# Up-to-down seams, opening orders and first combinations of a seven-product feed-forward kernel in exact-split fp32 on one core

## The reference

```
x = x + 1/2 * swiglu_ffn(rms(x)); x = x + mixer(rms(x)); x = x + 1/2 * swiglu_ffn(rms(x))   # per layer
swiglu_ffn(x) = (silu(gate) * up) @ w_out      with gate, up = split(x @ w_in), hidden width 2816
mixer of layer 0: pointwise projection + GLU, causal depthwise conv (31 taps), layer norm, swish, projection
mixer of layer 1: differential attention with rotary, over K and V computed from x after layer 0
y = rms(x)
```

## Time and profile before

| what | value |
|---|---|
| runs | 2136.56, 2140.81, 2141.0 us |
| profiled execution | 2139.42 us, its span 2137.6 us |
| PE busy | 1957.2 us (92%), 15236 matmuls |
| DVE, ACT, POOL busy | 1439.6 (67%), 868.9 (41%), 342.1 us (16%) |
| DMA | 340.70 MB, mean 159 GB/s |
| chain that ended last | PE 54%, DVE 24%, ACT 9%, issue 6%, DMA 5% |

### The profile page before, as it was taken

One profiled execution on the slowest core, in us unless ns is written; L12 is line 12 of the kernel. 1 busy time (PEld: TensorE's weight loads), 2 busy tenths in 40 slices (PEclk: granted clock), 3 DMA queues, 4 the chain that ended last, 5 costly groups with the idle time before them and its releaser, 6 DMA issues.

```text
span 2137.6 us, 36366 instructions
## 1 busy us (share of the span) xinstructions
PE 1957.2 (92%) x15236; PEld 1871.0 (88%) x15236; DVE 1439.6 (67%) x1739; ACT 868.9 (41%) x1235; POOL 342.1 (16%) x343
## 2 busy tenths in 40 slices
PE   4999899899789899899997999999988989998996
PEld 4989899888588899899997999899965779898996
DVE  6766757699867648566655747557678567567475
ACT  5423424455554324233344424333356445234242
POOL 1101000133121001011421001010421221010001
PEclk9999999999899999999999999999999999999998
DMA  9758566278457477573559568573676266584651
GB/s 265 165 148 216 139 171 157 78 158 168 92 143 192 115 191 169 151 196 81 155 147 244 134 171 194 158 177 90 190 227 227 79 159 147 165 219 119 176 146 55
DMA packets 318783, 340.70 MB, mean 159 GB/s; under 512 B 12163, under 2 KB 279812, under 8 KB 318476
## 3 DMA queue, kind: packets, MB, share of 16 engines
q1 hardware_dynamic: 275460, 216.97, 32.2%
q0 software_dynamic: 33840, 111.21, 27.7%
q10 hardware_dynamic: 9320, 10.20, 1.6%
HBM read 221.58 MB, written 7.53 MB: 107 GB/s over the span
## 4 chain that ended last, share of the span: by engine, by line
PE 54%; DVE 24%; ACT 9%; issue 6%; DMA 5%; ACTq 1%; POOL 0%; POOLq 0%; DVEq 0%; SPq 0%
PE ps_all L670 27%; PE ps_all L642 24%; DVE w_lo L1379 6%; ACT w_hi L999 4%; DVE conv_b L1655 2%; DVE t_gate L1502 2%; DVE conv L1655 2%; DMA raw<-w_out 1%; DMA raw_more_low<-raw_more_low 1%; DMA raw<-raw 1%; DVE xs_lo_low L1408 1%; DVE t_out L1533 1%; DVE t_gate L1446 1%; DVE hs_lo_low L1538 1%; DVE x L1611 1%
## 5 line engine op out<-in xcount | busy, mean ns | idle before, releaser
L670 PE MATMUL ps_all<-xs_hi_low,w_hi 128*128 128x260 f32 x1848 | 531.6, 288 | 60.1 <-DVE w_lo L1379 34.0
L670 PE MATMUL ps_all<-xs_hi_low,w_lo 128*128 128x260 f32 x1848 | 527.1, 285 | 0.0
L670 PE MATMUL ps_all<-xs_lo_low,w_hi 128*128 128x260 f32 x1848 | 524.7, 284 | 0.0
L999 ACT ACTIVATE w_hi<-raw 128x1024 fp32r<-128x1024 f32 (+1 forms) x252 | 259.0, 1028 | 463.8 <-PE ps_all L642 189.0
L670 PEld LDWEIGHTS ps_all<-xs_hi_low,w_hi 128*128 128x128 f32 x1848 | 352.2, 191 | 68.4 <-DVE w_lo L1379 41.2
L1379 DVE TENSOR_TENSOR w_lo<-raw,w_hi 128x1024 fp32r<-128x1024 f32 (+1 forms) x252 | 315.7, 1253 | 125.2 <-ACT w_hi L999 124.6
L670 PEld LDWEIGHTS ps_all<-xs_lo_low,w_hi 128*128 128x128 f32 x1848 | 352.3, 191 | 0.1
L670 PEld LDWEIGHTS ps_all<-xs_hi_low,w_lo 128*128 128x128 f32 x1848 | 352.0, 190 | 0.0
L999 ACT ACTIVATE w_hi<-raw_more_low 128x1024 fp32r<-128x1024 f32 x156 | 164.6, 1058 | 298.7 <-PE ps_all L670 194.6
L1379 DVE TENSOR_TENSOR w_lo<-raw_more_low,w_hi 128x1024 fp32r<-128x1024 f32 x156 | 192.3, 1238 | 104.1 <-ACT w_hi L999 103.8
L642 PE MATMUL ps_all<-hs_hi_low,w_hi 128*128 128x260 f32 x1056 | 222.2, 292 | 43.3 <-DVE hs_lo_low L1538 43.3
(11 more groups left out here) (251 smaller groups left out, 3624.7 us busy)
## 6 DMA issues: line engine op xcount, KB each, us to landing
raw_more_low<-w_in SPq DMA_DIRECT2D x105, 512.0 KB, 7.1
raw<-w_in SPq DMA_DIRECT2D x80, 512.0 KB, 6.1
raw_more_low<-raw_more_low POOLq DMA_DIRECT2D x72, 512.0 KB, 6.6
raw<-w_out SPq DMA_DIRECT2D x64, 512.0 KB, 4.8
raw<-raw POOLq DMA_DIRECT2D x60, 512.0 KB, 7.8
raw_more_high<-w_in SPq DMA_DIRECT2D x35, 512.0 KB, 7.0
raw<-w_out SPq DMA_DIRECT2D x32, 384.0 KB, 3.4
raw_more_high<-raw_more_high POOLq DMA_DIRECT2D x24, 512.0 KB, 6.4
```

The source lines that it names most:

```text
L670: mm = nc.tensor.matmul(ps_all[:, bank, 0:HALF], w[:, ring, j * GW + q * P:j * GW + (q + 1) * P], m, start=j == 0 and k == 0, stop=j == PA ...
L999: nc.scalar.activation(w_hi[:, n % RING, 0:width], src, ACT.Copy).then_inc(hi_made, 1)
```

## The change

1. **Down phases open with two tiles held back**: chunks 0 and 1 without their last two hidden tiles, then those two of each (`down_ramp`).
2. **The last group by token halves**: gate, Silu, product, high and low part run for the first 260 tokens between items 3 and 6, for the second behind item 6. `gate_first` moves ahead of `hidden_lo` and of `step(n + 3)` in all groups.
3. **First combinations in two places**: for FFN 0 pairs 1 and 3 use a second stage; squares, their sums and lambda move between the items of the first group.
4. **Orders**: `root` and `rms` of a fresh up phase move to items 3 and 4, the variance's PSUM to banks 0 and 1, so that item 5 waits for `rstd`; EARLY is 7; the last `step` of a down phase comes ahead of its drain; in `conv_out`, `o` and `v` the low part of a pair comes one step later; W12 of f=2's first group gets a buffer of its own and is loaded second.

```diff
-        ps_stat_up = ps_all[:, 6:8, 0:HALF]
+        ps_stat_up = ps_all[:, 0:2, 0:HALF]
...
+        stage_2, = over(XG + 108160, KD * T * 4, [("stage_2", [P, 8, HALF])])
+        w12_first, = over(XG + 62464, KD * P * 4, [("w12_first", [P, KD * P])])
+        def stage_of(s, j):
+            return stage_2 if s == 0 and j % 2 else stage
...
-                for blk in (W11, S3, S1, W22, W12) if first_in else (S3, S1, W22, W11, W12):
+                for blk in (W11, W12, S3, S1, W22) if first_in else (S3, S1, W22, W11, W12):
...
-        EARLY = 5
+        EARLY = 7
...
-                        if ph.kind == "up" and ph.part == 0 and ph.f == 2 and c == 4:
+                        if ph.kind == "up" and ph.part == 0 and ph.f == 2 and c == 5:
                             sp.wait_ge(chunk_used, ph.chunk0)
...
-                        hi, lo, ready = room.h_hi[:, k], room.h_lo[:, k], (h_ready, ph.h0 - ph.tiles + k + 1)
+                        hi, lo, ready = room.h_hi[:, k], room.h_lo[:, k], (h_ready, ph.h0 - ph.tiles + k // 2 * 2 + 2)
...
                     elif i == 5:
                         pe.wait_ge(p1_copied, ph.group0 + g + 1)
+                        if g == 0 and fresh(ph):
+                            pe.wait_ge(rstd_made, made + 1)
...
-                            if fresh(ph):
-                                variance(sums, (rstd_made, made) if made else None, ps_stat_up)
...
-                            if i == 3 and g == 0 and ph.part == 0:
-                                pe.wait_ge(rstd_made, made + fresh(ph))
-                                if ph.f == 2:
-                                    pe.wait_ge(v_copied, KD)
+                            if i == 3 and g == 0 and fresh(ph):
+                                variance(sums, (p1_copied, ph.group0 + 1), ps_stat_up)
+                            elif i == 3 and g == 0 and ph.part == 0:
+                                pe.wait_ge(v_copied, KD)
...
+                def down_ramp():
+                    early, late = range(ph.tiles - 2), range(ph.tiles - 2, ph.tiles)
+                    for tiles in (early, late):
+                        for c in range(2):
+                            chunk(ph, c, tiles=tiles)
...
+                first, second, last = slice(0, HALF), slice(HALF, T), ph.groups - 1
                 for g in range(ph.groups):
                     for i in range(ITEMS):
                         step(ph.chunk0 + ITEMS * g + i)
+                        if ph is phases[0] and g == 0:
+                            first_work(i)
                         if g and i == 1:
                             silu(g - 1)
                         elif g and i == 2:
                             hidden_hi(g - 1)
-                        elif not g and i == 1 and fresh(ph):
+                        elif not g and i == 3 and fresh(ph):
                             root(ps_stat_up)
+                        elif g == last and i == 4:
+                            silu(g, first, 1)
+                        elif g == last and i == 6:
+                            hidden_hi(g, first, 1)
                         if i == 1:
                             copy_p1(g)
-                silu(ph.groups - 1)
-                hidden_hi(ph.groups - 1)
+                silu(last, second, 1)
+                hidden_hi(last, second, 1)
...
+            def pair_before_lo(s, m):
+                if m and m % 2 == 0:
+                    combos_lo(s, m // 2 - 1, 0, 7, m // 2)
...
                     step(n + 1)
+                    if opening:
+                        first_work(1)
                     if g:
                         hidden(g - 1)
-                    elif fresh(ph):
-                        rms(ps_stat_up)
                     step(n + 2)
-                    if g:
-                        hidden_lo(g - 1)
-                    step(n + 3)
...
                     gate_first(g)
+                    if g:
+                        hidden_lo(g - 1)
+                    step(n + 3)
...
+                    if g == last:
+                        gate(g, first, 1)
                     step(n + 4)
+                    if g == 0 and fresh(ph):
+                        rms(ps_stat_up)
                     thirds(g)
                     step(n + 5)
                     up_second(g)
+                    if g == last:
+                        up_first(g)
+                        hidden(g, first, 1)
                     step(n + 6)
-                    up_first(g)
-                g = ph.groups - 1
-                gate_second(g)
-                gate(g)
-                hidden(g)
-                hidden_lo(g)
+                    if g == last:
+                        hidden_lo(g, first, 1)
+                    else:
+                        up_first(g)
+                gate_second(last)
+                gate(last, second, 1)
+                hidden(last, second, 1)
+                hidden_lo(last, second, 1)
...
-                    if m < KD - 1:
-                        step(n)
+                    step(n)
+                    if s in (2, 6):
+                        pair_before_lo(s, m)
                     dve.wait_ge(chunk_used, n + 1)
```

More of the change, by code:

```diff
@@ L434, in block_of @@
         def block_of(ph, g, block):
+            if ph.f == 2 and ph.part == 0 and g == 0 and block == W12:
+                return w12_first[:, :]
             return raw_of(ph, block + 5 * in_second(ph, g))
@@ L1063, in _, with first_work @@
             act.wait_ge(vec_in, 16)
[L1064 to L1069, removed]
-            round_hi(1)
[L1071 to L1078, removed]
+            act.wait_ge(x_in[0], 16)
+            copy_x(0, 0)
+            copy_x(0, 1)
+            act.wait_ge(x_in[1], 16)
+            copy_x(0, 2)
+            copy_x(0, 3)
+            combos_hi(0, 0, 0, 7, 4, 2)
+            round_hi(0)
+            combos_hi(0, 1, 0, 7, 4, 2)
+            act.wait_ge(x_in[2], 16)
+            pair_hi(0, 4)
+            pair_hi(0, 5)
+            round_hi(1)
+            act.wait_ge(x_in[3], 16)
+            pair_hi(0, 6)
+            pair_hi(0, 7)
+            def first_work(i):
+                if i < 2:
+                    for m in range(4 * i, 4 * i + 4):
+                        first_square(m)
+                elif i == 2:
+                    act.wait_ge(inputs, N_IN)
+                    nc.scalar.activation(ident_b[:, :], cst[:, C_ID:C_ID + P], ACT.Copy).then_inc(mask_made, 1)
+                    nc.scalar.activation(mask_b[:, :], cst[:, C_MASK:C_MASK + P], ACT.Copy).then_inc(mask_made, 1)
+                    act.wait_ge(lam_step, 2)
+                    nc.scalar.activation(lam_s[0:1, 2:4], lam_s[0:1, 0:2], ACT.Exp).then_inc(lam_step, 1)
+                    act.dma_start(new_state_d, state[:, 1:CW - 1, :]).then_inc(out_done, 16)
             def up(ph):
@@ L1143, in residual @@
                         continue
-                    if not final:
-                        step(ph.chunk0 + m)
+                    step(ph.chunk0 + m)
                     act.wait_ge(summed, sums + m - 1)
@@ L1536, in hidden_lo, with gate @@
-                def hidden_lo(g):
-                    dve.wait_ge(h_hi_made, ph.h0 + 2 * g + 2)
-                    nc.vector.tensor_tensor(room.h_lo[:, 2 * g:2 * g + 2, :], t_out[:, :, :], room.h_hi[:, 2 * g:2 * g + 2, :],
-                                            ALU.subtract).then_inc(h_ready, 2)
+                def gate(g, cols=slice(0, T), made=2):
+                    dve.wait_ge(taken, sums_of(ph, g, 1 if cols.start == 0 and made == 1 else 6))
+                    nc.vector.tensor_tensor(t_act[:, :, cols], t_gate[:, :, cols],
+                                            rstd[:, cols].unsqueeze(1).broadcast_to([P, 2, cols.stop - cols.start]), ALU.mult
+                                            ).then_inc(gate_made, made)
@@ L1541, in up @@
+                last = ph.groups - 1
                 for g in range(ph.groups):
-                    n = ph.chunk0 + ITEMS * g
+                    n, opening = ph.chunk0 + ITEMS * g, ph is phases[0] and g == 0
                     step(n)
+                    if opening:
+                        first_work(0)
                     if g:
```

119 lines of the change are left out of this document (67 added, 52 removed).

## The result

The changed kernel takes 2051.75 us (median of four runs, 2050.07 to 2054.74), the kernel before 2140.1 beside it: a ratio of 0.9592, 95% interval 0.9575 to 0.9608. Forecast were 2045, range 2031 to 2076. The profiled execution has a span of 2050.5 us, 87.1 less.

A forecast was written before the change was run, and what follows sets the result against it. TensorE was taken to bound the kernel, so only its waits and low clock could be won. Gains of 53.5 + 13.8 + 16.5 + 9.0 + 2.0 + 1.0 = 95.8 us gave 2043.6, by the median 2045; range 2031 to 2076.

The forecast's parts named there:

- Part 1: Eight seams into eight-tile down phases: two-chunk opening and token halves remove PE's wait and the low clock, 53.5 us gained.
- Rival A: At the seams the halves come too late, 1.5 us each, low clock in half: 27 us more, 2072; chance 0.20.
- Part 2: Four seams into six-tile down phases: 7.8 us gained at the first three, 6.0 at the last, 13.8 in sum.
- rival B: Split before drain costs: pair phases lose 4 each, three six-tile ends get nothing from EARLY (3 x 2): 2060; chance 0.12.
- Part 3: Every group of the up phases: `gate_first` moved ahead removes PE's wait at item 4, 16.5 of 17.5 us gained.
- Part 4: Opening of f=2: W12 in its own buffer is loaded earlier, so item 3 starts earlier, 9.0 us gained.
- Part 5: Opening of f=0: items 2 and 3 start earlier, item 5 waits 3.4 us for the root; net 2.0 us gained.
- Part 6: Openings of f=1 and f=3, with pair combinations completed one step later: net 0.5 us gained each, 1.0 in sum.
- Part 7: End of down phases without pairs: the last weight step ahead of the drain gains nothing, 1.2 us of cover gone each.
- Rival C: Up-phase groups run at the pace of block loads and DMA additions, so the kernel gets slower: 2150; chance 0.03.
- D: Nothing changes, because the early block is held by the last group all the same: 2139; chance 0.02.

## Why the prediction was right, and where it was not

The time, its sign and the mechanism held: 95.8 us were forecast, 87.1 came. By phases:

- **Part 1, 53.5: measured 55.0.** The count gave a chain that ends with the cover; it ended 0.2 before it. Rival A (halves too late) is out: no wait is left at the twelve seams. The runs without one part show what each did: the opening cures the clock, the halves the last 1.1 to 1.5 us. As for "VectorE: DVE Perf Modes", errata section, of the Trainium skill, the 520-element halves pay the fixed cost that it states (two of 0.70 against one of 1.24: 0.15 a pair), and still win 14 us, since only one half's chain is left behind the last sum.
- **Part 2, 13.8: measured 9.8** (9.1 + 5.9 - 5.2). Both sizes were right. x's last sum came 1.87 later for the forecast 1.8, and 2.43 + 1.87 - 1.44 is 2.86, the wait measured. The step that failed is the end of the sum: I did not price the clock at this wait. In k and q it fell, where it had not at 2.43; that is the half of rival B that came true: it asked 2 more at each of three ends, 7 in all with the 1.1 that the forecast itself gave away there; 5.2 came, of which the scatter of attention leaves a microsecond or two open. The window at the wait at the start of k, in the kernel before (wait 2.43), beside those of the changed kernel above (2.86):

```profile
1030.00:1032.00 2.00, 1.59 (x10) 1.47 (x11) 1.58 (x2) 1.97 (x3) 0.00 (x0) 1.00 0.28 114
```

  The split that began beside GpSimd's sum took 1.53 for eight tiles (1.23 alone; it began at 394.25, GpSimd's sum ran from 393.35 to 394.71), so the sum held it up. "Advanced Engine Details and Errata" of the Trainium skill, section "GPSIMD Details", has GpSimd conflict with VectorE instructions that have two SBUF inputs; this split has two, and the trace agrees.
- **Parts 3 to 6, 28.5: measured 22.3** (15.3 + 11.2 - 4.2). Part 3 was mis-sized to the low side: 16.5, and 20.7 when undone. So the rest, 12.0, brought 2 at most. That the sum is nearer than its parts is luck: what part 3 gave beyond its forecast covers 4 of the 10 that parts 4 to 6 lack. W12's buffer and the first combinations were not undone alone; what they brought is read from the phases.
 - *Part 4, 9.0: about nothing.* The opening of f=2 gained 2.5, all of it in its three later groups, which is part 3's; its first group took 34.5 us for 34.1. "GpSimd goes on to add W11 and S1 at about 1127 ... some 6.5 us" failed twice. I priced the pair order for conv_out and o alone and forgot that V has it too: its chunk 6 was drained 4.9 us late and GpSimd waited for it. And I took the sums' duration from a stretch with the queues free; beside the five loads they took 12.1. With V's order undone item 3 follows 14.0 behind V, near the forecast 12.6.
 - *Part 5, 2.0: about -1.* The marks were near (variance 39.4 for 38.5, item 5 waits 2.5 for 3.4), but the first group ended 1.0 later than before (58.75 for 57.76), and the phase gained 1.8, where 3.5 were due with its share of part 3. As in part 2 the clock was not priced, here behind the new waits of 6.11 for the variance and 2.54 for `rstd` (before, one such stretch from 42 to 46, behind 3.06):

```profile
40.00:42.00 2.00, 2.00 (x8) 1.71 (x7) 1.97 (x5) 0.41 (x3) 0.00 (x0) 0.50 1.01 199
...
52.00:54.00 2.00, 2.00 (x11) 2.00 (x10) 2.00 (x3) 0.00 (x0) 0.01 (x1) 0.50 0.98 335
```

 - *Part 6, 1.0: about -2.* The pitch is 14.12 for the forecast 14.3, item 5 waits 1.85 for 2; but conv_out and o lost 4.2 and the openings gave 7.0, over 4 of them part 3's. Undone, the order of these two phases changed nothing in the time (4.0 against 4.6).
- **Part 7, nothing:** it held where an up phase follows; no wait shows there.

Rival C is out: no wait for weights inside a group came back. D is out.

## What to carry to other kernels

When a producer's chain is late at a seam, give the consumer work of two outputs that does not need it, and measure the cover against the chain: here 8.7 against 8.5 us. An instruction moved ahead of another is right only for the queue that waits at that place: the same move gained in front of one kind of phase and lost in front of another, so it should be set per phase. A DMA duration holds for the queues as they were; ask what the change issues at the same moment.

## What was not expected of the hardware

In the profiles, PE stood 1.54 and 1.64 us at seams and 0.95 at one without loss of clock, and 2.90, 3.94 and 4.33 with it; but in the kernel before 2.43 us cost nothing in k and q and came with the half clock in conv_in, at the same place of the phase:

```profile
422.00:424.00 2.00, 2.00 (x11) 2.00 (x11) 1.50 (x3) 1.98 (x3) 0.00 (x0) 0.50 0.84 236
```

Behind a wait of 2.86 (k, changed kernel) the granted clock read 0.74, 0.50 and 0.91 in the next windows of 2 us. And block sums by DMA took 7.5, 8.5 and 12.1 us for the same bytes, by what SyncE had issued in the meantime.
